# Differential attention heads: two scaled maps and a sum, in place of one scaled map and a multiply-add

## What is computed

```python
def attend(qb, keys, vals):
    s = jnp.einsum('bqhmd,bkhmd->bhmqk', qb, keys).astype(f32) * ATTN_SCALE
    p = jax.nn.softmax(s, axis=-1)
    a = p[:, :, 0] - lam * p[:, :, 1]
    return jnp.einsum('bhqk,bkhe->bqhe', a.astype(vals.dtype), vals)
```

## Time and profile before

| | |
|---|---|
| median of 3 runs | 2826.0 us (2824.38 to 2826.77) |
| the profiled execution | 2822.39 us, of which the span of its instructions is 2820.0 us |
| PE busy | 2731.4 us (97% of the span) |
| DVE busy | 1629.0 us (58%) |
| ACT busy | 1135.7 us (40%) |
| POOL busy | 242.5 us (9%) |
| granted TensorE clock, mean | 0.990 |
| the differential heads | about 1988 to 2407 us of the span |

### The profile page before, as it was taken

How to read it: one execution, slowest core, us unless ns; L and a number is a source line. 1 busy time by engine, 2 the same in 40 slices (tenths; PEclk the granted TensorE clock), 3 DMA queues, 4 the chain that set the end, 5 groups by cost and what they waited for, 6 DMA issues and landing times.

```text
span 2820.0 us, 38289 instructions
## 1 busy us (share of the span) xinstructions
PE 2731.4 (97%) x14052; PEld 2265.8 (80%) x14052; DVE 1629.0 (58%) x2483; ACT 1135.7 (40%) x1774; POOL 242.5 (9%) x312
## 2 busy tenths in 40 slices
PE   8999999999999999999999999999999997899998
PEld 7888888888888878888777788887788886778776
DVE  6666466665656454442476544424667677367775
ACT  5222156654322142231455423223455555244553
POOL 0000000000000020000020000000122122021111
PEclk9999999999999999999999999999999999999999
DMA  5445421223444433333211333332111120111212
GB/s 175 138 130 148 132 75 52 57 56 111 127 138 138 148 105 92 99 92 104 79 38 38 98 97 94 99 96 76 51 51 48 52 57 27 52 49 38 53 38 67
DMA packets 332459, 240.78 MB, mean 85 GB/s; under 512 B 9424, under 2 KB 310608, under 8 KB 332240
## 3 DMA queue, kind: packets, MB, share of 16 engines
q1 hardware_dynamic: 321168, 205.50, 24.8%
q0 software_dynamic: 11200, 34.09, 4.3%
HBM read 231.96 MB, written 2.10 MB: 83 GB/s over the span
## 4 chain that ended last, share of the span: by engine, by line
PE 88%; DVE 6%; ACT 4%; issue 2%; POOL 0%; DMA 0%; ACTq 0%; DVEq 0%; SPq 0%; POOLq 0%
PE ps L457 25%; PE ps L458 25%; PE ps L459 25%; PE ps L771 2%; PE ps L1141 2%; PE ps L1296 2%; ACT apr L1991 1%; PE ps L1114 1%; PE ps L886 1%; DVE wl L452 1%; PE ps L890 1%; DVE tmp L506 1%; DVE bw_pt_l L2677 1%; DVE act_l L2188 1%; DVE x L2243 1%
## 5 line engine op out<-in xcount | busy, mean ns | idle before, releaser
L457 PE MATMUL ps<-act_h,wl 128*128 128x512 f32 x2224 | 888.9, 400 | 14.2 <-DVE act_l L2188 8.9
L459 PE MATMUL ps<-act_h,wh 128*128 128x512 f32 x2224 | 869.2, 391 | 0.0
L458 PE MATMUL ps<-act_l,wh 128*128 128x512 f32 x2224 | 869.0, 391 | 0.0
L452 DVE TENSOR_TENSOR wl<-raw,wh 128x1024 fp32r<-128x1024 f32 x382 | 466.2, 1235 | 351.4 <-ACT wh L448 348.8
L448 ACT ACTIVATE wh<-raw 128x1024 fp32r<-128x1024 f32 x382 | 393.9, 1052 | 469.8 <-PE ps L459 373.5
L457 PEld LDWEIGHTS ps<-act_h,wl 128*128 128x128 f32 x2224 | 419.3, 189 | 106.1 <-DVE wl L452 9.4
L459 PEld LDWEIGHTS ps<-act_h,wh 128*128 128x128 f32 x2224 | 419.0, 188 | 89.2
L458 PEld LDWEIGHTS ps<-act_l,wh 128*128 128x128 f32 x2224 | 419.6, 189 | 85.7 <-issue 4.3
L457 PE MATMUL ps<-h_h,wl 128*128 (+1 forms) x704 | 278.4, 396 | 0.0
L458 PE MATMUL ps<-h_l,wh 128*128 (+1 forms) x704 | 278.4, 396 | 0.0
L459 PE MATMUL ps<-h_h,wh 128*128 (+1 forms) x704 | 278.4, 396 | 0.0
(11 more groups left out here) (328 smaller groups left out, 3842.3 us busy)
## 6 DMA issues: line engine op xcount, KB each, us to landing
raw<-in_ffn_w_gate_up SPq DMA_DIRECT2D x176, 512.0 KB, 4.1
raw<-in_ffn_w_down SPq DMA_DIRECT2D x88, 512.0 KB, 3.8
raw<-in_a_w_in SPq DMA_DIRECT2D x32, 512.0 KB, 4.3
wmod<-in_w_mod POOLq DMA_DIRECT2D x48, 256.0 KB, 3.2
xc<-in_w_mod POOLq DMA_DIRECT2D x48, 256.0 KB, 3.3
raw<-in_sb_w_in SPq DMA_DIRECT2D x24, 512.0 KB, 4.0
raw<-in_b_w_in SPq DMA_DIRECT2D x20, 512.0 KB, 4.0
raw<-in_w_o SPq DMA_DIRECT2D x16, 512.0 KB, 4.0
```

What stands on the lines that cost most here:

```text
L452: dve.tensor_tensor(wl[:, slot, :], raw[:, slot % RAWS, :], f32(wh[:, slot, :]), ALU.subtract).then_inc(lo_done[slot], 1)
L457: pe.matmul(bank, w_lo, r_hi, start=start, stop=False, skip_group_check=skip)
L458: pe.matmul(bank, w_hi, r_lo, start=False, stop=False, skip_group_check=skip)
L459: return pe.matmul(bank, w_hi, r_hi, start=False, stop=stop, skip_group_check=skip)
```

## The change

`combine` multiplies map 0 by its factor in an instruction of its own, put ahead of the product of map 1, and the multiply-add becomes a plain sum. No wait and no semaphore is added or taken away: the sum still waits for pn0, which the product of map 1 raises.

```diff
                     dve.wait_ge(w.rc1, START + n)
+                    dve.tensor_scalar(apr[:, 0, 0:W], apr[:, 0, 0:W], st_nm[:, 0, 2:3], None, ALU.mult)
                     dve.tensor_scalar(apr[:, 1, 0:W], apr[:, 1, 0:W], st_nm[:, 1, 2:3], None,
                                       ALU.mult).then_inc(w.pn0, 1)
                     dve.wait_ge(w.pn0, START + n)
-                    dve.scalar_tensor_tensor(apr[:, 0, 0:W], apr[:, 0, 0:W], st_nm[:, 0, 2:3],
-                                             apr[:, 1, 0:W], ALU.mult, ALU.add).then_inc(w.pn, 1)
+                    dve.tensor_tensor(apr[:, 0, 0:W], apr[:, 0, 0:W], apr[:, 1, 0:W], ALU.add).then_inc(w.pn, 1)
```

## The result

| | before | after |
|---|---|---|
| median of 20 runs | 2824.7 us (2820.7 to 2826.9) | 2831.6 us (2827.2 to 2833.4) |
| the profiled execution, and its span | 2822.4 us, 2820.0 us | 2832.7 us, 2830.9 us |
| DVE busy | 1629.0 us | 1647.4 us |
| granted TensorE clock, mean | 0.990 | 0.986 |

The changed kernel is slower: its time is 1.0022 of the time before, with a 95% interval of 1.0016 to 1.0028. That is 6.2 us, with 4.5 to 7.9 us as the interval. The forecast was +3.5 us with a range of -1 to +8 us. So the sign and the range held, but the size came out nearer to the clock rival (+7.6 us) than to the forecast, and the interval lies across the 0.2% that the prediction took for what a measurement can tell from no change.

A forecast was written before the change was run, and what follows sets the result against it. PE, with 88% of the chain, was taken to bound the kernel, so DVE work counts only where PE waits. Head 7's 0.2 + 1.0 + 1.4 + 1.0 us, taken as 3.5, gave 2829.5 us; range 2825.0 to 2834.0 us.

The forecast's parts named there:

- clock rival: Head 7: POOL's turns count fully and TensorE's clock falls in two more stretches, +7.6 us, 2833.6 us; chance 0.08.
- price of a step alone, W = 768: DVE without POOL in the way: added product less overlap, plus sum, less multiply-add, 0.48 us more per 768-column step.
- head 7, step 0 (`v_lo`): PE's transposes start right behind `v_lo` after idle time, so the added 0.21 us come through: +0.2 us.
- step 2: Head 7: POOL comes in between the two products and ahead of the sum, which ends 1.0 us later.
- steps 3 and 4: Head 7: of 1.0 us, 0.60 are covered ahead of `p_hi`; 0.4 go on and 1.0 is added: +1.4 us.
- the scaling behind the maximum of step 5: Head 7: two numbers took 0.72 us in POOL's way; up to 0.5 us may go, but it was left in.
- step 5: Head 7: PE waits 3.29 us for the combine and nothing covers the delay, +1.0 us.
- up to the transposes of step 5: Head 7: its steps sum to 3.6 us, or 3.5 with a small part of the 0.5 us off.
- the clock behind them: TensorE's slow stretches in head 7: one or two more, or one fewer, -1.6 to +3.2 us, only in the range.
- looped heads: Heads 1 to 6: slack of 1.09 and 0.55 us covers prices of 0.48 and 0.21, so nothing on the path.
- POOL's turns: Head 7: DVE and POOL alternate whole instructions, making a step cost +1.0 us; without this, +0.48.
- two signs to look for: Head 7: PE's waits for the sum up from 6.7 to about 10 us; a sum of about 1.7 to 2.5 us.

The follow-up runs named there:

- clean pair: The kernel before and the changed kernel, each with one unused SBUF column declared: 2807.7 us and 2816.3 us, medians 8.5 us apart.
- E2: The kernel before with the change in heads 0 to 6 only, head 7 keeping its multiply-add: 2824.6 us, 1.0000 of before.
- E9: The changed kernel with an unread DVE maximum over 160 columns ahead of each combine of heads 1 to 6, its target a new SBUF column: 2815.7 us, 0.9969 of before.
- E10: The changed kernel with an unread DVE maximum over 768 columns ahead of each combine of heads 1 to 6, its target a new SBUF column: 2822.8 us, 0.9990 of before.
- E3: The kernel before with each of POOL's final_lo waiting until a combine of head 7 is done: 2823.4 us, 0.9998 of before.
- E4: The changed kernel with each of POOL's final_lo waiting until a combine of head 7 is done: 2825.8 us, 0.9998 of before.
- E7: The kernel before with POOL's final_lo work left out, empty instructions in its place: 2824.1 us, 0.9997 of before.
- E8: The changed kernel with POOL's final_lo work left out, empty instructions in its place: 2822.0 us, 0.9996 of before.
- E6: The changed kernel with six PE products of constants ahead of the transposes of step 5 of head 7: 2827.4 us, 1.0008 of before.
- E1: The kernel before with the change in head 7 only: 2831.9 us against 2825.1, a ratio of 1.0020.
- E5: The kernel before with six PE products of constants ahead of the transposes of step 5 of head 7: 2825.1 us, 1.0002 of before.
- E11: The kernel before with one unused SBUF column declared and no instruction changed: 2807.7 us in 5 runs, 0.9942 of before.
- E12: The changed kernel with one unused SBUF column declared and no instruction changed: 2816.3 us, 0.9969 of before.

## Why the prediction was right, and where it was short

| step of the prediction | forecast | measured |
|---|---|---|
| price of a step alone, W = 768 | 0.48 us | 0.47 us |
| DVE's work in all | +18.7 us | +18.4 us |
| heads 1 to 6 | 0 | 0.05 us; 0.00 in the clean pair |
| head 7, step 0 (`v_lo`) | +0.2 | +0.2 |
| step 2 | +1.0 | +1.0 |
| steps 3 and 4 | +1.4 | +1.3 |
| the scaling behind the maximum of step 5 | 0, up to -0.5 left open | -0.55 |
| step 5 | +1.0 | +1.0 |
| up to the transposes of step 5 | 3.5 | 3.0 |
| the clock behind them | 0 in the centre, -1.6 to +3.2 in the range | +2.6 |

The measured column comes from the rows of both kernels; the after times are 5.94 us later at the end of head 6. `v_lo`: 2359.58 against 2353.42, 6.16 us. The combine of step 2 starts 6.14 and ends 7.15 us later (2375.75 against 2368.60). The combine of step 3 starts 6.92 us later and ends 7.91 us later, but `p_hi` of step 3 only 7.35 us later (2385.21 against 2377.86), so of the 1.0 us of step 3 0.43 came through, forecast 0.4. The maximum of step 5 is 8.45 us later (2392.21 against 2383.76). The scaling behind it took 0.17 us and not 0.72, since POOL's turn no longer fell on it, which leaves 7.90. The sum's end, and with it the transposes of step 5, are 8.90 us later (2400.17 against 2391.27).

**Right: the looped heads.** The slack of 1.09 us at step 5 and 0.55 at step 0 covered the price; E2 and E9 confirm it, and E10 shows that it isn't endless.

**Right: POOL's turns.** The order of the pieces in step 2 held to 0.02 us, and E3, E4, E7 and E8 show that the added length goes when POOL goes. Here POOL got in between two DVE instructions that had no wait between them. The Trainium skill, "SBUF — State Buffer", section "Who interferes with whom", has the rule of the exclusive lock. The trace agrees with it for the products, the multiply-add and the sum, which work in SBUF alone, and for the maximum, which reads PSUM and stayed at 1.75 us in all kernels.

**Short: the clock.** The step that was short is the term for the clock, which stood at nothing in the centre and only in the range, with a chance of 0.08 for its upper part. It measured +2.6 us; E6 shows that it hangs on the idle time. I argued that behind the longest idle time, 3.29 us, the six transposes had still run at the fast level. That was true of the kernel before, and not of one whose idle time there is 4.51 us. Two rows around the point were at hand: behind 1.73 us of idle time the transposes of step 3 took 1.54 us, so neither the length of one wait nor its place told the level. Those rows left the level open at each of the waits. That a change which makes the waits longer more likely adds a slow stretch than not is a judgement after the fact: all six traces with the longest waits have one, but E3 and E4 have one too, behind short waits. With the 2.4 us of the two windows above, the centre would have been 3.5 + 2.4 = 5.9 us. That the measured 6.2 us fell inside the range is owed to the range's term for the clock, and in part to luck: the prediction argued against a slow stretch behind step 5.

**Short: two signs to look for.** PE's waits for the sum were to go to about 10 us and went to 8.4. The wait ahead of step 2 went from 1.65 to 1.20 us, because PE came later to it from work in a slow stretch. And the sum in head 7 was to take 1.7 to 2.5 us and took 1.36: by my own times, 2368.19 for the end of the product and 2369.59 for that of the sum, it had to be 1.4. The ends were right, and the recorded length I got from nothing.

What stays open: the 0.7 us of head 0, a slow stretch of the clock there that is twice as long. It is in all eight traces whose head 0 has the edit, and in E1, E3, E5 and E7, whose head 0 hasn't; it is missing in the kernel before and in E11 alone. The runs don't say whether the change has a part in it.

## What to carry to other kernels

Splitting a fused multiply-add costs a whole pass on DVE, 0.47 us here for 768 columns, and the 42 steps of heads 0 to 6 didn't notice; ask step by step how much slack stands behind the instruction, and add up only those where the next engine is waiting already. Where a wait of PE is going to grow, give the clock a price in the centre of the estimate and not only in the range: here 3.0 us on the path became 5.6. And a control kernel for any experiment that declares a tensor isn't a luxury, since a column that nobody reads moved the time by nearly three times what was being measured (16.8 us against 6.2).

## What the runs showed of the hardware

- **POOL comes in between two back-to-back DVE instructions**, and the instruction behind pays even if it has only two numbers a row: that scaling took 0.17 us alone, and 0.41, 0.72, 0.96 and 1.18 us in POOL's way.
- **A fall of the granted clock goes with PE's idle time, but the length of the last wait alone doesn't tell it.** Ahead of the transposes of step 5 PE waited, and the transposes then took:

| kernel | wait for the combine, us | six transposes, us | clock in 16 us | PE busy in them, us |
|---|---|---|---|---|
| before | 3.29 | 0.88 | 0.98 | 12.70 |
| E2 | 3.30 | 0.88 | 0.99 | 12.83 |
| E11 | 2.62 | 0.87 | 0.99 | 12.78 |
| E5, filled | 0.71 | 0.87 | 0.99 | 12.80 |
| E6, filled | 1.89 | 0.87 | 0.98 | 12.84 |
| E7 | 3.24 | 0.87 | 0.89 | 14.26 |
| E8 | 3.67 | 1.54 | 0.89 | 14.28 |
| E3 | 0.63 | 1.54 | 0.88 | 14.38 |
| E4 | 2.20 | 1.52 | 0.89 | 14.30 |
| E9 | 4.31 | 1.54 | 0.85 | 14.88 |
| E10 | 4.31 | 1.54 | 0.85 | 14.92 |
| E12 | 4.32 | 1.54 | 0.85 | 14.89 |
| E1 | 4.48 | 1.54 | 0.84 | 15.08 |
| changed | 4.51 | 1.54 | 0.83 | 15.09 |

  The six longest waits, 3.67 to 4.51 us, each had transposes at 1.2 GHz behind them, and of the eight shorter ones E3's, the shortest, and E4's; in E7 the clock fell right behind the transposes. Six products put into the idle time of the changed kernel brought the 2.4 GHz back (E6). A slow stretch here cost 1.5 to 2.4 us. Each row is one trace.
- **Gains of a microsecond or two ahead of such a point can be given back behind it.** In head 7 E3 reached step 5 1.8 us earlier, and E7 2.9 us earlier, than the kernel before; neither ended measurably earlier.
- **Where tensors lie in SBUF can change the pace of a product.** 396 and 389 ns for the same products, tensors 4 bytes apart. That is 13.5 us by the products, and the medians of the whole kernel are 16.8 us apart.
